# Expert stage: copying both halves of the next block's weights behind Silu and the gated product

## The chip, the cores and the metric

The kernel runs on one core of one Trainium2 chip. The metric is the device time of the whole program in microseconds, the median of the runs; the profile is that of one further execution. Engines are named as in the profile: PE is TensorE, DVE VectorE, ACT ScalarE, POOL GpSimd and SP SyncE, whose queue issues most transfers.

## The reference, cut to what matters

The program is one block of a hybrid model: four mixers over 1024 tokens of width 1024, and behind them a layer of 64 experts. The change is in the experts. A router picks 8 of 64 experts for each token. Each expert is a gated feed-forward with a hidden width of 256:

```python
def swiglu(t, wg, wu, wd):
    return (jax.nn.silu(t @ wg) * (t @ wu)) @ wd
```

`wg` and `wu` are 1024 x 256 (gate and up), `wd` is 256 x 1024 (down), all in float32. The tokens are sorted by expert and computed in blocks, and the results are weighted and summed per token later on.

## The kernel before

**Blocks.** The stage `experts` (L3086) works through 80 blocks (`NBLK`) of 128 rows. Each block has 4 sub-blocks of 32 rows, and each sub-block belongs to one expert, so a block can need the weights of up to four experts. Tables in SBUF, made from the routing in an earlier stage, give for each sub-block the ring slot of its gate and up weights, how many experts must have been loaded, and the ring slot of its down weights.

**Weights.** SyncE loads the experts in order into a ring of 3 slots for gate and up (2 MB per expert) and a ring of 4 for down (1 MB). It refills a gate-and-up slot once the copies out of it are done (`hi_d`, `hi_a`) and TensorE has read it (`up`). One sub-block of a block (number 3) is computed by TensorE straight from the ring. For the other three the weights are first copied within SBUF to fixed buffers (`WC`, `WDC`). The gate and up copies of a block are cut into a low half (contraction chunks 0 to 3) and a high half (chunks 4 to 7). VectorE copies sub-blocks 0 and 1 (L3408 and L3409 low, L3415 and L3416 high), ScalarE sub-block 2 (L3345 low, L3351 high). GpSimd copies the down weights of three sub-blocks (L3214) once TensorE has finished `widen` of the block before. There is one set of these buffers, so the low half may be overwritten only when TensorE is through the low chunks of the block that uses it (`half_up`), and the high half when it is through all of them (`up`).

**The engines' queues.** Every engine works in the order in which its code stands, and semaphores tie the engines together. For a step that ends block b0 and works on b1 behind it:

- TensorE (L3296): `hidden(b1)` makes the gate and up products of a block (L3253, L3255), 16 groups of four matmuls, with a wait for the high copies in front of its second eight; `widen(b0)` the down products (L3284, L3287); `fold(b1)` turns the hidden rows (L3270); `turn(b3)` turns the gathered rows of a later block (L3238). `hidden` also waits for the low copies and for the weights' arrival.
- ScalarE (L3353): `low(b2)`, `silu(b1)` (L3326), `high(b2)`, then `store(b0)` (L3331 and the store's issue at L3334), `fold(b1)` (L3338), and half of the scaled copies of turned rows, `flat_half(b3)` (L3320).
- VectorE (L3418): `low(b2)`, `gated(b1)` (L3396, Silu's result times the up product), `high(b2)`, `store(b0)` (L3401), `flat_half(b3)` (L3386), `index(b5)` (L3392).
- GpSimd (L3201): `copy_down` of the next block, then the indirect gather of rows of a later block (L3204), which waits for `index`.

`low` begins with register work: `slot_of` and `count_of` (L3117 to L3122) read the tables into registers of the engine, two slots and one count on VectorE, one of each on ScalarE. Then it waits for the experts' arrival and for `half_up`, and then it copies.
Of the kernel before, what the change touches and what calls it, by code (L numbers as in the profile page):

```python
# [63 lines left out]
def hold(eng, sem, value):  # L64

    eng.wait_ge(sem, value)
    if not isinstance(value, int):
        eng.nop(nofuse=True)  # L68
# [3017 lines left out]
def experts(nc, k, ctx, cr, wg, wu, wd, xn_dram, y_dram, TAB, END, IDX):  # L3086
# [30 lines left out]
    def slot_of(eng, b, u):  # L3117
        n = eng.value_load(TAB[0:1, bass.ds(b.n * SUB + u if u else b.n * SUB, 1)], min_val=0, max_val=RING - 1)
        return bass.ds(n, 1)

    def count_of(eng, b, u):
        return eng.value_load(TAB[0:1, bass.ds(b.n * SUB + (u + NTAB * P), 1)], min_val=1, max_val=NE)  # L3122
# [5 lines left out]
    def part_of(slot, cs):  # L3128
        return WGU[:, slot, :, cs, :].rearrange("p a g c n -> p (a g) (c n)")

    def copy_of(u, cs):
        return WC[:, u, :, cs, :].rearrange("p g c n -> p g (c n)")
# [7 lines left out]
    with nc.Block() as block:  # L3140
# [174 lines left out]
        @block.scalar  # L3315
        def _(act):
            def flat_half(b):
                hold(act, turned, b.n + 1)
                for c in range(KC // 2):
                    last = nc.scalar.activation(XTT[:, b.q, c], ps[0][:, c * P:(c + 1) * P], ACT.Identity,  # L3320
                                                bias=k.add_col[1][0][:, c:c + 1], scale=k.mul_col[1][0][:, c:c + 1])
                last.then_inc(xa, 1)

            def silu(b):
                hold(act, up, b.n + 2)
                nc.scalar.activation(SG[:, b.q], ps[2 + b.q][:, 0:ED], ACT.Silu).then_inc(sil, 1)  # L3326

            def store(b):
                hold(act, dn, b.n + 2)
                hold(act, st[b.q], b.half * 16 + 16)  # L3330
                nc.scalar.copy(YB[:, b.q, 0:512], ps[6][:, :]).then_inc(ya, 1)  # L3331
                hold(act, ya, b.n + 2)
                hold(act, yd, b.n + 2)
                act.dma_start(y_dram[bass.ds(b.n * P, P), :], YB[:, b.q]).then_inc(st[b.q], 16)  # L3334

            def fold(b):
                hold(act, ht, b.n + 1)
                nc.scalar.copy(HT[:, b.q], ps[4][:, 0:2 * P].rearrange("p (f n) -> p f n", f=2)).then_inc(hto, 1)  # L3338

            def low(b, n=1):  # L3340
                slot = slot_of(act, b, 2)
                hold(act, arrived, count_of(act, b, 2))
                if n:
                    hold(act, half_up, b.n)
                nc.scalar.copy(copy_of(2, LOW), part_of(slot, LOW)).then_inc(lo_a, 1)  # L3345
                return slot

            def high(b, slot, n=1):
                if n:
                    hold(act, up, b.n + 1)  # L3350
                nc.scalar.copy(copy_of(2, HIGH), part_of(slot, HIGH)).then_inc(hi_a, 1)  # L3351

            def step(b0, b1, b2, b3):  # L3353
                if b2 is not None:
                    slot = low(b2)
                silu(b1)
                if b2 is not None:
                    high(b2, slot)
                store(b0)
                fold(b1)  # L3360
                if b3 is not None:
                    flat_half(b3)

            high(Turn.at(0), low(Turn.at(0), 0), 0)
            flat_half(Turn.at(0))
            flat_half(Turn.at(1))
            slot = low(Turn.at(1))
            silu(Turn.at(0))
            high(Turn.at(1), slot)
            fold(Turn.at(0))  # L3370
            flat_half(Turn.at(2))
            with act.Fori(0, TRIPS - 1) as t:
                for off in range(2):
                    step(Turn(t, off), Turn(t, off + 1), Turn(t, off + 2), Turn(t, off + 3))
            for n in range(NBLK - 4, NBLK - 1):
                step(Turn.at(n), Turn.at(n + 1), *(Turn.at(n + d) if n + d < NBLK else None for d in (2, 3)))
            store(Turn.at(NBLK - 1))
            act.wait_ge(st[0], 16 * (TRIPS + 2))
            act.wait_ge(st[1], 16 * (TRIPS + 2))

        @block.vector
        def _(dve):
            def flat_half(b):
                hold(dve, turned, b.n + 1)
                for c in range(KC // 2, KC):
                    last = nc.vector.tensor_scalar(XTT[:, b.q, c], ps[1][:, (c - 4) * P:(c - 3) * P],  # L3386
                                                   k.mul_col[1][0][:, c:c + 1], k.add_col[1][0][:, c:c + 1],
                                                   ALU.mult, ALU.add)
                last.then_inc(xd, 1)

            def index(b):
                nc.vector.tensor_copy(ID[:, b.q], IDX[:, bass.ds(b.n, 1)]).then_inc(idx, 1)  # L3392

            def gated(b):
                hold(dve, sil, b.n + 1)
                nc.vector.tensor_tensor(H[:, b.q], SG[:, b.q], ps[2 + b.q][:, ED:], ALU.mult).then_inc(hid, 1)  # L3396

            def store(b):
                hold(dve, dn, b.n + 2)
                hold(dve, st[b.q], b.half * 16 + 16)  # L3400
                nc.vector.tensor_copy(YB[:, b.q, 512:], ps[7][:, :]).then_inc(yd, 1)  # L3401

            def low(b, n=1):
                slots = [slot_of(dve, b, u) for u in (0, 1)]
                hold(dve, arrived, count_of(dve, b, 1))
                if n:
                    hold(dve, half_up, b.n)
                nc.vector.tensor_copy(copy_of(0, LOW), part_of(slots[0], LOW))  # L3408
                nc.vector.tensor_copy(copy_of(1, LOW), part_of(slots[1], LOW)).then_inc(lo_d, 1)  # L3409
                return slots  # L3410

            def high(b, slots, n=1):
                if n:
                    hold(dve, up, b.n + 1)
                nc.vector.tensor_copy(copy_of(0, HIGH), part_of(slots[0], HIGH))  # L3415
                nc.vector.tensor_copy(copy_of(1, HIGH), part_of(slots[1], HIGH)).then_inc(hi_d, 1)  # L3416

            def step(b0, b1, b2, b3, b5):  # L3418
                if b2 is not None:
                    slots = low(b2)  # L3420
                gated(b1)
                if b2 is not None:
                    high(b2, slots)
                store(b0)
                if b3 is not None:
                    flat_half(b3)
                if b5 is not None:
                    index(b5)

            index(Turn.at(0))  # L3430
            index(Turn.at(1))
            high(Turn.at(0), low(Turn.at(0), 0), 0)
            flat_half(Turn.at(0))
            index(Turn.at(2))
            flat_half(Turn.at(1))
            index(Turn.at(3))
            slots = low(Turn.at(1))
            gated(Turn.at(0))
            high(Turn.at(1), slots)
            flat_half(Turn.at(2))  # L3440
            index(Turn.at(4))
            with dve.Fori(0, TRIPS - 1) as t:
                for off in range(2):
                    step(*(Turn(t, off + d) for d in (0, 1, 2, 3, 5)))
            for n in range(NBLK - 4, NBLK - 1):
                step(*(Turn.at(n + d) if n + d < NBLK else None for d in (0, 1, 2, 3, 5)))
            store(Turn.at(NBLK - 1))
# [202 lines left out]
```

## Time and profile before

| | us |
|---|---|
| median of 3 runs | 3009.71 (3006.03 to 3025.67) |
| the profiled execution | 3010.0 |
| its span | 3008.3 |
| TensorE matmul busy | 2621.9 (87%) |
| VectorE busy | 1537.0 (51%) |
| ScalarE busy | 983.5 (33%) |
| GpSimd busy | 829.3 (28%) |

The span runs from the first to the last instruction. Busy shares are averages over all stages; the expert stage covers the last third of the span but its end. Within it a line of the timeline is one instruction, or several of the same kind in a row, with its start counted from the start of the span. What an engine waited for stands in brackets.

### The profile page before, as it was taken

What the parts mean: (1) busy time and instruction counts of PE and PEld (TensorE: products, weight loads), DVE (VectorE), ACT (ScalarE), POOL (GpSimd) and SP (SyncE); (2) the same over time, 40 slices, a digit from 0 to 9 for tenths busy, and PEclk for the clock granted to TensorE, in tenths of its full rate; (3) what the DMA queues carried; (4) which work ended last, traced back from release to release, by engine and by line L of the source; (5) the groups of instructions that cost most, each with busy time, mean ns of one, the idle gap of its engine ahead of it and who ended that gap; (6) DMA issues with size and microseconds to landing.
All of it is one profiled execution on the core that took longest, in us unless ns stands there. A gap on an engine that the chain in (4) does not pass through costs nothing. (4 is left out here: it accounts for less than half of the span.)

```text
span 3008.3 us, 78943 instructions
## 1 busy us (share of the span) xinstructions
PE 2621.9 (87%) x30395; PEld 1471.1 (49%) x30396; DVE 1537.0 (51%) x2779; ACT 983.5 (33%) x1687; POOL 829.3 (28%) x654
## 2 busy tenths in 40 slices
PE   5998899798899698788969797898889998999956
PEld 2447368355788544788844352332333333333322
DVE  3116276553466504344444386565556655666628
ACT  3513127213222022222211113453445544555511
POOL 1000000001333000111100002565456555666565
PEclk9999999899999899999979898998999999999978
DMA  6001302300000100000022207787878887873167
GB/s 241 0 0 62 111 14 85 102 15 1 3 4 4 51 18 1 3 4 4 4 100 84 102 8 286 286 313 289 310 300 317 315 303 292 304 286 145 77 268 319
DMA packets 109130, 408.57 MB, mean 136 GB/s; under 512 B 21001, under 2 KB 37083, under 8 KB 83932
## 3 DMA queue, kind: packets, MB, share of 16 engines
q1 hardware_dynamic: 76636, 287.71, 26.2%
q0 software_dynamic: 20736, 75.51, 6.6%
q10 hardware_dynamic: 11520, 41.95, 3.5%
q8 instruction: 178, 2.92, 0.4%
q14 instruction: 60, 0.49, 0.0%
HBM read 346.40 MB, written 58.72 MB: 135 GB/s over the span
## 5 line engine op out<-in xcount | busy, mean ns | idle before, releaser
L3253 PE MATMUL bank<-arena 128*32 x1280 | 584.0, 611 | 45.7 <-SPq L68 36.1
L3255 PE MATMUL bank<-arena 128*32 128x512 f32 x3840 | 585.1, 611 | 0.0
L3214 POOL COPY arena<-arena 128x2048 f32 x240 | 456.4, 1935 | 392.3 <-PE bank L3287 390.8
L1341 PE MATMUL bank<-arena 64*64 64x64 f32 x8320 | 279.1, 220 | 69.7 <-DVE arena L1437 19.7
L3253 PEld LDWEIGHTS bank<-arena 128*32 128x32 f32 x1280 | 137.3, 112 | 408.6 <-issue 400.7
L1341 PEld LDWEIGHTS bank<-arena 64*64 64x64 f32 x8320 | 261.8, 136 | 81.5 <-DVE arena L1437 22.4
L3284 PE MATMUL bank<-arena 128*32 x640 | 290.3, 597 | 5.5 <-POOL arena L3214 5.5
L3287 PE MATMUL bank<-arena 128*32 128x512 f32 x1920 | 291.3, 597 | 0.0
L3408 DVE COPY arena<-arena 128x2048 f32 x80 | 130.7, 1633 | 262.2 <-PE bank L3255 204.6
L3345 ACT COPY arena<-arena 128x2048 f32 x80 | 152.0, 1901 | 277.2 <-PE bank L3255 160.0
L3204 POOL DMA_INDIRECT arena<-normed_rows,arena x80 | 152.4, 1906 | 163.5 <-DVE arena L3392 152.1
L3284 PEld LDWEIGHTS bank<-arena 128*32 128x32 f32 x640 | 70.6, 110 | 198.8 <-issue 198.7
L3255 PEld LDWEIGHTS bank<-arena 128*32 128x32 f32 x3840 | 152.7, 112 | 0.0
L3351 ACT COPY arena<-arena 128x2048 f32 x80 | 151.9, 1899 | 0.0
L2478 POOL TENSOR_TENSOR arena<-arena 128x512 f32<-128x512 f32 x10 | 12.8, 1283 | 463.5 <-DVE arena L2536 463.5
L1435 DVE TENSOR_TENSOR arena<-arena,bank 128x512 f32<-128x512 f32 x100 | 68.8, 688 | 123.9 <-PE bank L1341 115.7
L1575 PE MATMUL bank<-arena 128*128 128x512 f32 (+1 forms) x320 | 129.5, 565 | 0.3 <-PE bank L1575 0.3
L3386 DVE TENSOR_SCALAR arena<-bank,arena 128x128 f32<-128x128 f32 x320 | 109.2, 403 | 36.8 <-PE bank L3238 36.8
L497 PE MATMUL bank<-arena 128*128 128x512 f32 (+1 forms) x320 | 127.3, 552 | 0.0
L2748 PE MATMUL bank<-arena 128*128 128x512 f32 x256 | 115.0, 608 | 9.7 <-ACT arena L2770 8.5
L3320 ACT ACTIVATE arena<-bank,arena 128x128 f32<-128x128 f32 x320 | 120.8, 465 | 3.3 <-PE bank L3238 3.3
L1456 DVE SCALAR_TENSOR_TENSOR arena<-arena 128x945 f32<-128x945 f32 (+2 forms) x96 | 113.8, 1220 | 1.7
(561 smaller groups left out, 4438.9 us busy)
## 6 DMA issues: line engine op xcount, KB each, us to landing
arena<-in_exp_w_gate_dram SPq DMA_DIRECT2D x64, 1024.0 KB
arena<-in_exp_w_up_dram SPq DMA_DIRECT2D x64, 1024.0 KB
arena<-in_exp_w_down_dram SPq DMA_DIRECT2D x64, 1024.0 KB
expert_rows<-arena ACTq DMA_DIRECT2D x80, 512.0 KB
arena<-in_w_mod_dram SPq DMA_DIRECT2D x32, 512.0 KB, 9.8
arena<-in_x_dram SPq DMA_DIRECT2D x16, 512.0 KB, 7.7
arena<-in_w_mod_dram SPq DMA_DIRECT2D x8, 1024.0 KB, 17.7
arena<-in_w_in_dram SPq DMA_DIRECT2D x12, 384.0 KB
```

Of the source, the lines that this page charges most:

```text
L497: last = nc.tensor.matmul(k.ps[p % 4][:, 0:width], k.hT[:, c, t * P:(t + 1) * P], W[g][:, c, ws], start=(c == 0), stop=(c == KC - 1))
L1341: last = self.nc.tensor.matmul(self.banks[bank][r, x * HD:(x + 1) * HD], lhsT[r, x], rhs[r, x], start=True, stop=True)
L1575: last = nc.tensor.matmul(k.ps[p % 4][:, 0:w], W[m // 3 % 2][:, c, (m % 3) * P:(m % 3 + 1) * P], k.hT[:, c, a:a + w], start=(c == 0), stop ...
L3204: nc.gpsimd.indirect_dma_start(out=G[:, b.q], out_offset=None, in_=xn_dram, in_offset=bass.IndirectOffsetOnAxis(ap=ID[:, b.q], axis=0)).th ...
L3214: last = nc.gpsimd.tensor_copy(down_copy(u), down_of(slots[u]))
L3253: nc.tensor.matmul(out(SUB - 1), XTT[:, b.q, c, rows(SUB - 1)], W[:, :, c], start=first, stop=end)
L3255: last = nc.tensor.matmul(out(u), XTT[:, b.q, c, rows(u)], WC[:, u, :, c], start=first, stop=end)
L3284: nc.tensor.matmul(ps[6 + half][rows(SUB - 1), :], HT[:, b.q, f, rows(SUB - 1)], W[:, f, c], start=(f == 0), stop=(f == 1))
L3287: last = nc.tensor.matmul(ps[6 + half][rows(u), :], HT[:, b.q, f, rows(u)], WDC[:, u, f, c], start=(f == 0), stop=(f == 1))
L3345: nc.scalar.copy(copy_of(2, LOW), part_of(slot, LOW)).then_inc(lo_a, 1)
L3351: nc.scalar.copy(copy_of(2, HIGH), part_of(slot, HIGH)).then_inc(hi_a, 1)
L3408: nc.vector.tensor_copy(copy_of(0, LOW), part_of(slots[0], LOW))
```

## The change

On both engines the step called `low(b2)` first, kept the slots it returned, did `silu(b1)` or `gated(b1)`, and then called `high(b2, slots)`. Now `silu(b1)` or `gated(b1)` comes first, and `high(b2, low(b2))` behind it. The same is done in front of the loop. What `low` and `high` do is unchanged: the register reads, the waits and the copies move together.

```diff
@@ ScalarE
             def step(b0, b1, b2, b3):
-                if b2 is not None:
-                    slot = low(b2)
                 silu(b1)
                 if b2 is not None:
-                    high(b2, slot)
+                    high(b2, low(b2))
                 store(b0)
                 fold(b1)
@@
-            slot = low(Turn.at(1))
             silu(Turn.at(0))
-            high(Turn.at(1), slot)
+            high(Turn.at(1), low(Turn.at(1)))
             fold(Turn.at(0))
@@ VectorE
             def step(b0, b1, b2, b3, b5):
-                if b2 is not None:
-                    slots = low(b2)
                 gated(b1)
                 if b2 is not None:
-                    high(b2, slots)
+                    high(b2, low(b2))
                 store(b0)
@@
-            slots = low(Turn.at(1))
             gated(Turn.at(0))
-            high(Turn.at(1), slots)
+            high(Turn.at(1), low(Turn.at(1)))
             flat_half(Turn.at(2))
```

## Rows read from the trace of the kernel before

**Rows 1.** TensorE's timeline: start us, us, engine, line, operation, count

```profile
1845.45 1.06 PE L3253 MATMUL bank<-arena 128*32 x1
...
2246.34 0.62 PE L3253 MATMUL bank<-arena 128*32 x1
...
2249.80 0.59 PE L3253 MATMUL bank<-arena 128*32 x1
...
2252.81 0.60 PE L3255 MATMUL bank<-arena 128*32 128x512 f32 x3
...
2258.11 0.62 PE L3253 MATMUL bank<-arena 128*32 x1
...
2858.33 0.62 PE L3253 MATMUL bank<-arena 128*32 x1
```

**Rows 2.** Waits in the expert stage: us in total, times, longest us

```profile
PE bank L3253 <- SPq L68: 36.1, 6, 9.6
...
PE bank L3270 <- DVE arena L3396: 17.3, 5, 6.6
```

**Rows 3.** TensorE's timeline behind two gaps

```profile
2015.86 0.61 PE L3253 MATMUL bank<-arena 128*32 x1 [1.66 <-issue]
...
2367.19 0.61 PE L3253 MATMUL bank<-arena 128*32 x1 [3.07 <-SPq L68]
...
2368.06 1.05 PE L3253 MATMUL bank<-arena 128*32 x1
```

**Rows 4.** Busy time by window: us, PE, PEld, DVE, ACT, POOL, PEclk, DMA share, GB/s

```profile
2369.00:2371.00 2.00, 2.00 (x16) 0.58 (x12) 0.00 (x0) 0.00 (x0) 0.80 (x1) 0.50 0.88 324
```

**Rows 5.** VectorE's timeline in the step of rows 1

```profile
2250.23 1.83 DVE L3408 COPY arena<-arena 128x2048 f32 x1 [2.27 <-PE bank L3255]
...
2254.03 0.42 DVE L3396 TENSOR_TENSOR arena<-arena,bank 128x256 f32<-128x256 f32 x1 [0.84 <-ACT arena L3326]
2254.37 1.22 DVE L3415 COPY arena<-arena 128x2048 f32 x1
2255.50 1.22 DVE L3416 COPY arena<-arena 128x2048 f32 x1
...
2259.58 0.15 DVE L3392 COPY arena<-arena 128x1 int32 x1
```

**Rows 6.** ScalarE's timeline in the same step

```profile
2250.20 1.90 ACT L3345 COPY arena<-arena 128x2048 f32 x1 [1.77 <-PE bank L3255]
2253.55 0.38 ACT L3326 ACTIVATE arena<-bank 128x256 f32<-128x256 f32 x1 [1.45 <-PE bank L3255]
```

**Rows 7.** GpSimd's timeline in the same step

```profile
2257.11 5.56 POOL L3214 COPY arena<-arena 128x2048 f32 x3 [3.79 <-PE bank L3287]
```

**Rows 8.** VectorE's queue, first and last register record of three steps; ns min/median/max

```profile
L3118 DVEq ALU_OP  x1: 40/40/40, 2247.3 to 2247.3; - x1
L3122 DVEq SEQ_ASSERT  x1: 23/23/23, 2249.9 to 2249.9; - x1
...
L3118 DVEq ALU_OP  x1: 40/40/40, 2294.4 to 2294.4; - x1
L3122 DVEq SEQ_ASSERT  x1: 23/23/23, 2296.5 to 2296.5; - x1
...
L3118 DVEq ALU_OP  x1: 40/40/40, 2497.1 to 2497.1; - x1
L3122 DVEq SEQ_ASSERT  x1: 23/23/23, 2500.7 to 2500.7; - x1
```

**Rows 9.** Timeline: GpSimd's and VectorE's copies side by side; a late copy

```profile
1849.56 7.55 POOL L3214 COPY arena<-arena 128x2048 f32 x3 [1.52 <-SPq L3185]
...
2038.63 2.82 DVE L3408 COPY arena<-arena 128x2048 f32 x1 [9.38 <-SPq L68]
...
2501.05 1.23 DVE L3408 COPY arena<-arena 128x2048 f32 x1 [3.25 <-issue]
```

**Rows 10.** SyncE's waits in the expert stage: us in total, times, longest

```profile
SPq L68 <- DVE arena L3416: 21.5, 3, 7.7
```

## The prediction, made before the changed kernel was run

> **What bounds the kernel now.** I read the groups by line first: the costliest lines belong to the expert stage. Then the stage's ends: TensorE's first product of the first block starts at 1845.45, that of the last of 80 blocks at 2858.33, so 79 steps from block to block take 1012.9 us [rows 1]. Then one undisturbed step, engine by engine. `hidden` starts at 2246.34 and again at 2258.11, 11.77 us later, and TensorE has no gap in between: 7.07 us of `hidden` to the end of its last products (2252.81 + 0.60 = 2253.41), then `widen`, `fold`, `turn` [rows 1]. A step is TensorE's; 79 x 11.77 = 929.8 us. The other 83.1 us lie in steps whose weights came late. The list of waits has 36.1 us of them as TensorE waiting for the queue that announces weights [rows 2]; the slow clock behind a gap is another part [rows 3, 4].
>
> I count time from the end of `hidden` (2253.41 = 0). VectorE's low copies start at -3.18, behind the first half of `hidden`; ScalarE's Silu at 0.14, VectorE's gated product at 0.62, its high copies at 0.96, done at 3.31 [rows 5, 6]. GpSimd's three copies start at 3.70 and take 5.56 [rows 7]. `hidden` of the next block starts at 4.70 and wants the low copies then, the high ones 3.46 later (its ninth group, 2249.80 against 2246.34), at 8.16 [rows 1]. Now the high copies are 4.85 us early, the low ones as much or more.
>
> **The change part by part.** No instruction is added; one wait, on the first half of `hidden`, is asked later and is then always met. Moved is `low`: two copies on VectorE, one on ScalarE, and the register work ahead of them (reads of slot numbers and counts from the table). The queues of TensorE, GpSimd and SyncE keep their order.
>
> *Silu and gated product* start where they do now, since they wait for the end of `hidden`. `fold` comes at 3.4, so in an undisturbed step an earlier product brings nothing. With late weights it does: TensorE waited 17.3 us in 5 steps for a product [rows 2], held up behind late low copies. That is all there is to gain.
>
> *Register work.* VectorE's runs from 2247.3 to 2249.9, 2.6 us, under the idle time before its copy, which starts 0.33 later at 2250.23 [rows 5, 8]. In another step it took 2.1 us, in a third 3.6 us; in this third VectorE stood idle for 3.25 us with only this to wait for, and the copy started 0.35 behind its last record [rows 8, 9]. After the change the work stands behind the wait for Silu and starts about with the gated product, beside its 0.42 us. Bounds 2.1 and 3.6; I take 2.6, the length in the step I follow. The first low copy asks at 0.62 + 2.6 + 0.33 = 3.55.
>
> *Copies beside GpSimd's.* A VectorE copy alone takes 1.22 us, the next one starting 1.13 behind it [rows 5]. Beside GpSimd's it took 2.82, and GpSimd's three took 7.55 for 5.56 [rows 7, 9]. Turn by turn fits both: a GpSimd copy is 5.56 / 3 = 1.85, and one of VectorE's behind it some 1.0, together 2.85; three of GpSimd's with two of VectorE's between them are 5.56 + 2.0 = 7.56. So I take it that whichever asks first goes first. Sharing in proportion would make every VectorE copy last 2.85 from 3.70 on: low copies done near 9.1, `hidden` from 9.2, a step of 9.2 + 7.07 + 1.7 for the clock (below) = 18.0.
>
> The Trainium skill ("SBUF — State Buffer", Who interferes with whom) says that a VectorE copy of this kind and a GpSimd operation exclude each other for a whole instruction, the one that issues first going first. By that rule, the trace agrees, with the 7.55; a model of shared bandwidth would give the 18.0.
>
> By turns: the first low copy asks at 3.55, before GpSimd's 3.70, and ends at 4.68. Then GpSimd and VectorE alternate: second low copy done at 7.53, high ones at 10.38 and 13.23; GpSimd's last at 12.23.
>
> *TensorE.* `hidden` starts at 7.6 for 4.70, a gap of 2.9. Its first half ends at 7.6 + 3.46 = 11.1 and waits for the high copies to 13.23; with 0.14 for the handover, as Silu shows [rows 6], it resumes at 13.4, and the second half takes 3.61 (2249.80 to 2253.41) [rows 1]. The next end is at 17.0: a step grows by 5.23.
>
> *TensorE's clock.* Behind a gap of 3.07 us the granted clock fell to 0.50, the 1.2 GHz level, and groups took 1.05 us for 0.59; there are four such, 0.85 apart for 0.43, so 1.7 us [rows 3, 4]. Behind a gap of 1.66 the group that starts `hidden` took its usual 0.61 [rows 3]. The new gap is near the upper one. If the clock falls, the first half ends at 12.8, still ahead of 13.4: I cost it at nothing. Its cover is the wait for the high copies; without that it is 1.7 per step.
>
> *ScalarE.* Silu to 0.5, register work, two copies of 1.90 [rows 6]: even with 3.6 us of register work both end by 8.3, inside VectorE's 13.23. Its store issue waits for VectorE's store at about 14, and the folded hidden rows behind that, by 15, are wanted by `widen` at 17.0. It holds.
>
> *Tails.* VectorE's store, scaled copies and index end 3.0 behind the high copies (2259.58 + 0.15 against 2256.72) [rows 5], near 16.3 and so before the next 17.0. GpSimd's gather waits for that index instead of following its copies at once; its rows are wanted two steps later. Nothing.
>
> *Weights.* SyncE refills a slot once its high copies are done, now 10 us later in a step. It has waited for them in 3 places only, 21.5 us in all [rows 10]: refills set their own pace, and blocks now come 5 us slower. Of the 83.1 us of late weights between 0 and 83.1 stay. I take 10: the lower end is nearer, but several small experts in a row can still outrun three slots.
>
> *Sum:* 79 x 5.23 = 413, less 83.1 - 10 = 73: +340 us. On the profiled execution (3010.0 us, span 3008.3; 0.3 from the median, 3009.7) that is **3350 us**.
>
> **Rivals.**
> 1. *GpSimd first.* With 2.75 us or more of register work the first low copy asks after 3.70. Low copies are then done at 6.55 and 9.40, high ones at 12.25 and 13.4; `hidden` starts at 9.5, a gap of 4.8, and its end is at 9.5 + 7.07 + 1.7 = 18.3. 79 x 6.5 - 73 = +440: 3450 us. For it: a margin of only 0.15, and a step with 3.6 us. Against it: the 2.1 [rows 8]. Chance 0.20. Sharing in proportion gives 79 x 6.2 - 73 = +417, 3427 us; against it stands the 7.56 for 7.55. Chance 0.06.
> 2. *Register work half hidden* (0.8 to 1.9 us). Both low copies are through before 3.70, and the first high copy waits for GpSimd: high ones done at 3.70 + 2 x 2.85 = 9.4 for 8.16, a step of 13.2. 79 x 1.4 = 111, less some 70 of weight waits: 3050 us. No step that I read shows under 2.1. Chance 0.10.
> 3. *The other side: register work for nothing.* If it were done while VectorE waits for Silu, low copies would run from 1.05, the first high copy would ask ahead of 3.70, and the last would end at 7.4, before 8.16. It decides at a first low copy at 1.4. Steps stay 11.77, and the 17.3 us go: 2993 us. For it: the queue runs half a microsecond ahead of the engine, whose index copy of that step comes 11.77 before 2259.58, at 2247.8, behind the start of the register work at 2247.3 [rows 5, 8]. Against it: a wait stands ahead of it now. Chance 0.08, 0.02 of it for more than 1% faster.
> 4. *Worse:* the clock stays low in the second half too, or weights are as late as before on top of rival 1: over 3480. Chance 0.06.
>
> **How the numbers follow.** The forecast has 0.50; its own range is 3310 (register work 2.1, all 0.5 earlier: 79 x 0.5 = 40) to 3420 (all 83 us of weight waits stay). The range, 3240 to 3480, adds rival 1 and sharing; the lower end leaves room for an order that alternates with rival 2's. Left out are rivals 2 to 4, some 0.2. Within 1% (30 us, about what a measurement of this kernel can tell from no change) lies most of rival 3 alone: faster 0.02, same 0.06, slower 0.92.
>
> **What would show it.** First low copy at 3.5 behind the end of `hidden`, the reads behind the gated product; three of VectorE's four copies at 2.8 or more, GpSimd's three at 8.5 with the wait for the first; TensorE waiting 2.9 us ahead of `hidden` and 2.2 in its middle; steps of 17.0; hardly a wait for weights. It is wrong if the register work is over before 1.4, or if copies beside GpSimd's are not slowed; and by 100 us if GpSimd asks first.

## The result and the profile after

The changed kernel takes 3334.16 us (median of 4 runs, 3326.61 to 3341.46) against 3011.41 before: a ratio of 1.1065, 95% interval 1.1037 to 1.1092. The forecast was 3350 us. All the readings in this section are of the profiled execution, 3338.48 us with a span of 3336.8. One execution of one version below (one slot ahead) ran in a slow state, at 4617 us against 3157 to 3163 of its other three, and is left out of that version's time.

The page shows VectorE busy for 1867.6 us, 330.6 more than before, with the same number of instructions, and GpSimd for 935.9, 106.6 more; TensorE is busy for 2691.5. The groups of the page say where. The columns are those of the page: busy us and mean ns of one, then the idle time ahead of them and what ended it.

```profile
L3253 PE MATMUL bank<-arena 128*32 x1280 | 650.2, 659 | 317.6 <-DVE arena L3406 223.6
L3214 POOL COPY arena<-arena 128x2048 f32 x240 | 635.9, 2684 | 364.6 <-PE bank L3287 363.1
...
L3412 DVE COPY arena<-arena 128x2048 f32 x80 | 229.3, 2867 | 0.0
L3413 DVE COPY arena<-arena 128x2048 f32 x80 | 229.2, 2865 | 0.0
L3406 DVE COPY arena<-arena 128x2048 f32 x80 | 224.6, 2807 | 0.0
...
L3405 DVE COPY arena<-arena 128x2048 f32 x80 | 98.2, 1227 | 168.3 <-issue 156.2
```

The first low copy (L3405) takes 1.23 us, as a copy does alone. The other three take 2.81 to 2.87, and a copy of GpSimd's 2.68 for 1.85. In front of the first low copy VectorE stood idle for 156.2 us with nothing to wait for, 2.0 us a time: that is the register work. TensorE, which had no gap in an undisturbed step, stood idle for 317.6 us in front of `hidden` and within it.

One step shows it in order of time. VectorE's timeline:

```profile
2331.56 0.42 DVE L3393 TENSOR_TENSOR arena<-arena,bank 128x256 f32<-128x256 f32 x1 [2.79 <-ACT arena L3326]
2334.01 1.23 DVE L3405 COPY arena<-arena 128x2048 f32 x1 [2.03 <-issue]
2335.16 2.91 DVE L3406 COPY arena<-arena 128x2048 f32 x1
2337.99 2.91 DVE L3412 COPY arena<-arena 128x2048 f32 x1
2340.82 2.91 DVE L3413 COPY arena<-arena 128x2048 f32 x1
```

GpSimd's copies in that step:

```profile
2334.59 8.05 POOL L3214 COPY arena<-arena 128x2048 f32 x3 [4.11 <-PE bank L3287]
```

TensorE's timeline with the end of one `hidden` (its last group, started at 2330.21, ends at 2330.81) and the first and ninth group of the next:

```profile
2330.21 0.59 PE L3253 MATMUL bank<-arena 128*32 x1
...
2338.64 0.61 PE L3253 MATMUL bank<-arena 128*32 x1 [3.05 <-DVE arena L3406]
...
2344.08 0.61 PE L3253 MATMUL bank<-arena 128*32 x1 [1.80 <-DVE arena L3413]
```

Counted from the end of `hidden`, 2330.81: the product at 0.75, the first low copy at 3.20, GpSimd at 3.78, the second low copy done at 7.26, `hidden` from 7.83 instead of 4.70 [rows 1], the high copies done at 12.92. TensorE waits twice, 3.05 us and 1.80 us. The step from 2321.75, where the `hidden` before began, to 2338.64 is 16.89 us. Over the stage, `hidden` of the first block starts at 1845.18 and that of the last at 3184.51:

```profile
1845.18 1.05 PE L3253 MATMUL bank<-arena 128*32 x1
...
2321.75 0.61 PE L3253 MATMUL bank<-arena 128*32 x1 [2.76 <-DVE arena L3406]
...
3184.51 1.06 PE L3253 MATMUL bank<-arena 128*32 x1 [2.92 <-DVE arena L3406]
```

That is 1339.3 us for 79 steps, 326.4 more than before, of the 328.5 by which the two spans differ. The whole loss lies in the steps. The waits of the stage (us in total, times, longest) say what became of late weights. The first line is the wait ahead of `hidden`, the second the one in its middle, as far as the trace assigns it:

```profile
PE bank L3253 <- DVE arena L3406: 223.6, 75, 3.4
PE bank L3253 <- DVE arena L3413: 82.2, 46, 2.0
...
PE bank L3253 <- SPq L68: 9.1, 1, 9.1
```

TensorE's waits for the queue that announces weights fell from 36.1 us in 6 places [rows 2] to 9.1 in one. SyncE, on the other hand, waits far more for the high copies than before (21.5 us in 3 places [rows 10]), and hardly anyone waits for SyncE: the weights come faster than the blocks. From SyncE's list:

```profile
SPq L68 <- DVE arena L3413: 294.9, 38, 20.8
```

### The profile page after: what moved, and what is told of

Read it like the earlier page. It is cut to its first block and busy times, and to the rows that moved or that the text cites. A ratio compares the mean times of both kernels' runs of the same rounds, so it can differ in the third digit from the quotient of the medians.

```text
span 3336.8 us, 78905 instructions
## 1 busy us (share of the span) xinstructions
PE 2691.5 (81%) x30395; PEld 1474.4 (44%) x30396; DVE 1867.6 (56%) x2779; ACT 977.3 (29%) x1687; POOL 935.9 (28%) x654
## 3 DMA queue, kind: packets, MB, share of 16 engines
q8 instruction: 178, 2.92, 0.3%
## 5 line engine op out<-in xcount | busy, mean ns | idle before, releaser
L3253 PE MATMUL bank<-arena 128*32 x1280 | 650.2, 659 | 317.6 <-DVE arena L3406 223.6
L3214 POOL COPY arena<-arena 128x2048 f32 x240 | 635.9, 2684 | 364.6 <-PE bank L3287 363.1
L3255 PE MATMUL bank<-arena 128*32 128x512 f32 x3840 | 652.7, 659 | 0.0
L3284 PE MATMUL bank<-arena 128*32 x640 | 290.0, 596 | 8.1 <-POOL arena L3214 5.5
L3287 PE MATMUL bank<-arena 128*32 128x512 f32 x1920 | 291.1, 596 | 0.0
L3412 DVE COPY arena<-arena 128x2048 f32 x80 | 229.3, 2867 | 0.0
L3413 DVE COPY arena<-arena 128x2048 f32 x80 | 229.2, 2865 | 0.0
L3406 DVE COPY arena<-arena 128x2048 f32 x80 | 224.6, 2807 | 0.0
L3338 ACT COPY arena<-bank 128x256 f32<-128x256 f32 x80 | 29.8, 372 | 642.9 <-DVE arena L3398 642.9
L3204 POOL DMA_INDIRECT arena<-normed_rows,arena x80 | 77.3, 966 | 416.0 <-DVE arena L3389 415.7
L3405 DVE COPY arena<-arena 128x2048 f32 x80 | 98.2, 1227 | 168.3 <-issue 156.2
L3393 DVE TENSOR_TENSOR arena<-arena,bank 128x256 f32<-128x256 f32 x80 | 33.7, 421 | 246.9 <-ACT arena L3326 246.9
L1575 PE MATMUL bank<-arena 128*128 128x512 f32 (+1 forms) x320 | 129.6, 565 | 0.3 <-PE bank L1575 0.3
## 6 DMA issues: line engine op xcount, KB each, us to landing
arena<-in_w_mod_dram SPq DMA_DIRECT2D x8, 1024.0 KB, 18.3
```

Of the source, the lines that this page charges most:

```text
L1575: last = nc.tensor.matmul(k.ps[p % 4][:, 0:w], W[m // 3 % 2][:, c, (m % 3) * P:(m % 3 + 1) * P], k.hT[:, c, a:a + w], start=(c == 0), stop ...
L3214: last = nc.gpsimd.tensor_copy(down_copy(u), down_of(slots[u]))
L3253: nc.tensor.matmul(out(SUB - 1), XTT[:, b.q, c, rows(SUB - 1)], W[:, :, c], start=first, stop=end)
L3255: last = nc.tensor.matmul(out(u), XTT[:, b.q, c, rows(u)], WC[:, u, :, c], start=first, stop=end)
L3284: nc.tensor.matmul(ps[6 + half][rows(SUB - 1), :], HT[:, b.q, f, rows(SUB - 1)], W[:, f, c], start=(f == 0), stop=(f == 1))
L3287: last = nc.tensor.matmul(ps[6 + half][rows(u), :], HT[:, b.q, f, rows(u)], WDC[:, u, f, c], start=(f == 0), stop=(f == 1))
```

## The experiments

Theory A is the prediction's: the register work, moved behind the product, pushes VectorE's copies into the time of GpSimd's, and from there the two engines take turns, the one that asks first going first. All versions but two are made from the changed kernel; ScalarE's half alone and the last one are made from the kernel before. Times of the steps are medians over the steps of the profiled execution. The first low copy's start, the time at which GpSimd asks for its first copy, and the end of the last high copy are counted from the end of `hidden`.

| version | first low copy | GpSimd asks | high done | step | program | ratio to before |
|---|---|---|---|---|---|---|
| before | -3.2 | 3.7 | 3.3 | 11.8 | 3011 | 1 |
| all reads ahead | 1.0 | 3.8 | 7.3 | 12.0 | 3026.19 | 1.0032 (1.0019 to 1.0045) |
| two slots ahead | 1.6 | 3.8 | 8.8 (7.9 or 9.6) | 13.6 | 3072.04 | 1.0185 (1.0146 to 1.0223) |
| one slot ahead | 2.3 | 3.8 | 10.3 | 14.3 | 3158.90 | 1.0483 (1.0434 to 1.0532) |
| changed kernel | 3.2 | 3.8 | 12.9 | 16.9 | 3334.16 | 1.1065 (1.1037 to 1.1092) |
| VectorE later | 4.3 | 3.7 | 13.5 | 19.5 | 3523.25 | 1.1684 (1.1654 to 1.1714) |
| GpSimd later | 3.2 | 4.8 | 11.2 | 15.2 | 3208.35 | 1.0641 (1.0614 to 1.0669) |

Where reads or copies are moved, the diffs below show the lines in one engine's step; the same is done in front of the loop. `look_up` does the reads, and `low` then takes what it found.

**All reads ahead.** Only the register reads go back in front of Silu and the product, on both engines (the diff has VectorE's step); the copies stay where the change put them.

```diff
             def step(b0, b1, b2, b3, b5):
+                if b2 is not None:
+                    found = look_up(b2)
                 gated(b1)
                 if b2 is not None:
-                    high(b2, low(b2))
+                    high(b2, low(b2, 1, found))
```

> The changed kernel, but the register reads of slots and counts stand ahead of Silu and the gated product again; only the copies stay behind them. Theory A (the reads behind the product push the first low copy to about GpSimd's start, and from there the two engines take turns): without them the first low copy starts at about 1.05 us after the end of hidden, the first high copy asks ahead of GpSimd, the high copies are done by about 7.4, steps are 11.8 us again, and the program takes 2990 to 3020 us. Rival B (copies are slowed in proportion while GpSimd copies, whoever asks first): high copies done near 8.4, steps of 12.1, some 3030 us. Rival C (the copies are simply too late behind the product, and the reads hardly matter): steps near 16.9 and 3300 us or more.

3026.19 us, 1.0032 of the kernel before. VectorE's and GpSimd's timelines:

```profile
2417.43 0.42 DVE L3399 TENSOR_TENSOR arena<-arena,bank 128x256 f32<-128x256 f32 x1 [5.50 <-ACT arena L3326]
2417.76 1.22 DVE L3414 COPY arena<-arena 128x2048 f32 x1
2418.90 1.22 DVE L3415 COPY arena<-arena 128x2048 f32 x1
2420.04 1.22 DVE L3421 COPY arena<-arena 128x2048 f32 x1
2421.17 2.91 DVE L3422 COPY arena<-arena 128x2048 f32 x1
```

```profile
2420.51 7.16 POOL L3214 COPY arena<-arena 128x2048 f32 x3 [3.98 <-PE bank L3287]
```

The order that the change wanted, product first and both halves behind it, costs 10 us (3026.19 against 3015.89 for the kernel before on the same chip) instead of 323. The third copy asks 0.47 us ahead of GpSimd and goes through; only the fourth waits. The high copies are done at 7.3, as expected, before the 8.16 at which TensorE wants them. Rivals B and C fall. The program came out 6 us above the range of A: the gain that A allowed for late weights did not come, and steps are 12.0 us and not 11.77. Where these 0.2 us lie was not followed.

**One half of the change each.** VectorE's half alone (ScalarE copies its low half first, as before; the diff below), and ScalarE's alone (the kernel before with ScalarE's part of the change):

```diff
             def step(b0, b1, b2, b3):
-                silu(b1)
                 if b2 is not None:
-                    high(b2, low(b2))
+                    slot = low(b2)
+                silu(b1)
+                if b2 is not None:
+                    high(b2, slot)
```

> Only VectorE's half of the change: ScalarE copies its low half first, as before. Theory A: all of the loss is VectorE's, 3320 to 3345 us, steps of 16.9. Rival D (ScalarE's copy, now behind Silu, carries part of it): about halfway, near 3170 us.

> Only ScalarE's half of the change: VectorE copies its low half first, as before. Theory A: ScalarE's copies end by 6 us after the end of hidden and hide behind everything, so 2990 to 3020 us, at best 17 us under the kernel before, where Silu no longer stands behind a late low copy. Rival D: near 3170 us.

ScalarE's half alone takes 3024.13 us (1.0020, 1.0003 to 1.0037): it costs next to nothing, as A says, and brings nothing. But VectorE's half alone takes 3427.26 us (1.1355, 1.1333 to 1.1377), 93 us more than both together, where A and D allowed no more than 3345. Its steps alternate between 16.4 to 17.9 and 19.1 us. ScalarE's timeline in a step of 19.1, behind an end of `hidden` at 2596.7:

```profile
2593.53 0.35 ACTq L3334 DMA_DIRECT2D expert_rows<-arena  x1
...
2596.32 1.90 ACT L3345 COPY arena<-arena 128x2048 f32 x1 [0.55 <-issue]
2598.12 0.38 ACT L3326 ACTIVATE arena<-bank 128x256 f32<-128x256 f32 x1
```

ScalarE can issue its store only behind VectorE's, which now comes some 13.5 us after the end of `hidden`. Its own low copy and the reads before it therefore end late, and Silu, which stands behind the copy, starts 1.4 us after the end of `hidden` instead of 0.14. VectorE's timeline and GpSimd's in the same step:

```profile
2598.60 0.42 DVE L3396 TENSOR_TENSOR arena<-arena,bank 128x256 f32<-128x256 f32 x1 [3.96 <-ACT arena L3326]
2601.05 2.31 DVE L3408 COPY arena<-arena 128x2048 f32 x1 [2.03 <-issue]
```

```profile
2600.39 7.55 POOL L3214 COPY arena<-arena 128x2048 f32 x3 [4.02 <-PE bank L3287]
```

The first low copy asks 0.66 us behind GpSimd and loses the first turn: it is rival 1 of the prediction, in every second step (38 of 78; in 36 of them Silu started 0.9 us or more after the end of `hidden`). So ScalarE's half of the change is not free of effect: with VectorE's half in place it keeps Silu on time, and is worth 93 us.

**GpSimd's copies cut short.** This version leaves out most of the copying of the down weights: from the second block on, 128 of 2048 columns are copied, so the results are not those of the block, and only the time is of use.

```diff
+                c = slice(0, 128 if n else 2 * D)
                 for u in range(SUB - 1):
-                    last = nc.gpsimd.tensor_copy(down_copy(u), down_of(slots[u]))
+                    last = nc.gpsimd.tensor_copy(down_copy(u)[:, c], down_of(slots[u])[:, c])
```

> The changed kernel with GpSimd's copies of the down weights cut from 2048 to 128 columns per partition from the second block on (most of that work is left out). Theory A: VectorE's four copies all take 1.22 us, low ones done at 5.5 after the end of hidden, high ones at 7.8, steps of 12.6 us, 79 x 4.3 = 340 us less, with some waits for weights back: 3000 to 3050 us. Rival E (the later start alone costs the time, GpSimd has no part in it): 3300 us or more.

3086.22 us (two runs): 248 us less than the changed kernel, and 36 above the range. VectorE's four copies start at 3.1 and are done at 8.0, TensorE's wait in the middle is gone, and steps are 13.3 us. The 0.7 us over the expected 12.6 are an error of mine in the expectation: I took `hidden` to start as soon as the low copies end (5.5) but it starts at 6.2, some 0.6 us behind their end, as in the changed kernel. Of the 5.1 us per step GpSimd's part is therefore 16.9 - 13.3 = 3.6, and 1.5 remain for the later start alone. Rival E falls for the larger part and holds for that rest.

**Who asks first.** GpSimd made later by two more reads, and VectorE made later by two more:

```diff
                 if n:
                     hold(pool, dn, b.n + 1)
+                    for u in range(2):
+                        down_slot_of(pool, b, u)
```

```diff
                 if n:
                     hold(dve, half_up, b.n)
+                    for u in (0, 1):
+                        slot_of(dve, b, u)
```

> The changed kernel with two more register reads on GpSimd between its wait for the end of widen and its copies, so that it asks about 0.9 us later, at 4.6 us instead of 3.7 after the end of hidden. Theory A (turns; whoever asks first goes first): VectorE's second low copy asks at 4.3, ahead of GpSimd, low copies are done at 5.4, one copy of GpSimd's fewer stands before each later one, the high copies are done at 11.1, steps are 15.1 us and the program takes 3334 - 79 x 1.8 = 3190 us: faster through more work. Rival B (slowed in proportion): steps of 16.0, 3260 us. Rival E (GpSimd has no part): no change, 3334 us.

> The changed kernel with two more register reads on VectorE in front of its low copies, about 1.2 us, so that the first low copy asks at 4.4 us instead of 3.2 after the end of hidden, behind GpSimd's 3.7. Theory A: GpSimd goes first, low copies are done at 6.6 and 9.4, hidden starts at 9.5 with a gap that costs the clock 1.7 us, steps are 18.3 us: 3334 + 79 x 1.4 = 3445 us. Rival B (in proportion): low copies done at 10.1, steps of 19.0, 3500 us. Rival E (everything is simply moved by the added reads): 16.9 + 1.2 = 18.1, 3430 us; what tells it from A is the first low copy, 2.8 us in A and 1.2 in E.

*GpSimd later:* 3208.35 us, 126 us less than the changed kernel though each step does more. VectorE's timeline and GpSimd's:

```profile
2492.33 1.23 DVE L3407 COPY arena<-arena 128x2048 f32 x1 [2.01 <-issue]
2493.48 1.22 DVE L3408 COPY arena<-arena 128x2048 f32 x1
2494.61 2.91 DVE L3414 COPY arena<-arena 128x2048 f32 x1
2497.44 2.91 DVE L3415 COPY arena<-arena 128x2048 f32 x1
```

```profile
2494.06 8.04 POOL L3216 COPY arena<-arena 128x2048 f32 x3 [5.13 <-issue]
```

The second low copy is at work when GpSimd asks, and takes 1.22 us to its end, unslowed. With sharing in proportion (B) it would have slowed. The step is 15.2 us, against 15.1 in A and 16.0 in B, and the program 18 us above A's 3190 and 52 under B's 3260.

*VectorE later:* 3523.25 us. VectorE's first low copy and GpSimd's copies in one step:

```profile
2632.13 2.44 DVE L3407 COPY arena<-arena 128x2048 f32 x1 [3.27 <-issue]
```

```profile
2631.60 7.55 POOL L3214 COPY arena<-arena 128x2048 f32 x3 [5.16 <-PE bank L3287]
```

The first low copy asks at 4.3, behind GpSimd, and takes 2.44 us, in all 78 steps over 2 us. So GpSimd did go first and E falls. But A's 3445 us is 78 too low, and the time is nearer to B's 3500. The copies are A's, with the low ones done at 9.5 (9.4 in A, 10.1 in B) and the high ones at 13.5; the steps are 19.5 us and not the 18.3 of A. The rest is TensorE's timeline:

```profile
2637.98 1.06 PE L3253 MATMUL bank<-arena 128*32 x1 [5.40 <-DVE arena L3408]
2638.83 1.06 PE L3253 MATMUL bank<-arena 128*32 x1
...
2641.39 1.06 PE L3253 MATMUL bank<-arena 128*32 x1
2642.25 0.79 PE L3253 MATMUL bank<-arena 128*32 x1
```

Behind the gap of 5.40 us the first five groups take 1.06 us and start 0.85 apart, and a sixth is part slow: 5 x 0.42 + 0.2 = 2.3 us (1.3 to 2.9 in other steps), where I took 1.7 from the kernel before; and `hidden` starts at 10.1 for 9.5, of which the handover is again 0.57.

**Part of the reads ahead.** Two slot reads ahead of the product and the count behind it (the diff below); and one slot ahead, one and the count behind:

```diff
             def step(b0, b1, b2, b3, b5):
+                if b2 is not None:
+                    slots = look_up(b2)
                 gated(b1)
                 if b2 is not None:
-                    high(b2, low(b2))
+                    high(b2, low(b2, 1, slots))
```

> The changed kernel with VectorE's two slot reads ahead of the gated product; only the read of the count stays between the product and the copies. The first low copy should start at about 1.7 us after the end of hidden, between 0.95 (all reads ahead) and 3.2 (none). Theory A (turns): the low copies are through by 4.0, GpSimd has asked at 3.75, so the first high copy waits for one of its copies and the second for another: high ones done near 9.7 us, TensorE's wait moves from in front of hidden into its middle alone, steps of 13.6 us; with some 40 us of weight waits, 3115 us. Rival F (the loss grows evenly with the delay of the copies, 137 us per us of delay): 3129 us. The total does not tell them apart; the high copies do: 2.9 us each and done at 9.7 in A, at 8.1 in F (7.3 + 0.8).

> The same with one slot read ahead, one slot and the count behind: first low copy at about 2.4 us. Theory A (turns): both low copies have asked before GpSimd (second at 3.55, GpSimd at 3.75), so the count of turns is the same as with two slots ahead and everything is only 0.7 us later: high ones done at 10.4, hidden from 5.3, steps of 14.3 us, 3155 us. The step from here to the changed kernel is then the large one (180 us for 0.8 us of delay), since there the second low copy has lost its place. Rival F (evenly with the delay): 3225 us.

3072.04 and 3158.90 us. VectorE's and GpSimd's timelines with two slots ahead:

```profile
2450.00 1.23 DVE L3408 COPY arena<-arena 128x2048 f32 x1 [0.57 <-issue]
2451.14 1.22 DVE L3409 COPY arena<-arena 128x2048 f32 x1
2452.28 2.92 DVE L3415 COPY arena<-arena 128x2048 f32 x1
2455.12 2.91 DVE L3416 COPY arena<-arena 128x2048 f32 x1
```

```profile
2452.09 4.86 POOL L3214 COPY arena<-arena 128x2048 f32 x2 [4.02 <-PE bank L3287]
```

Here the third copy asks 0.19 us behind GpSimd and takes 2.92; with all reads ahead it asked 0.47 us ahead and took 1.22. With two slots ahead the order in fact falls both ways, and that is the sharpest test of who goes first. Of 78 steps, the third copy took 1.22 us in 39, and in each of these its record starts ahead of GpSimd's or at most 0.02 us behind it; in the other 39 it starts 0.03 us or more behind, and takes 2.9. The high copies are done at 7.9 in the first kind and at 9.6 in the second, and from one end of `hidden` to the next it is 12.1 and 13.6 us. So A's 13.6 us and 9.7 hold for half of the steps only. Rival F has the high copies done at 8.1 in every step and gives no two kinds. The shorter steps are worth 39 x 1.5 = 60 us, which is more than the 43 by which the program is faster than its sum. In them GpSimd asks at 4.1 (median) instead of 3.7; why was not followed.

With one slot ahead there is one kind only: the third copy is slow in all 78 steps, steps are 14.3 us and the high copies done at 10.3, as A had them (14.3 and 10.4), and the program is 4 us from its sum and 66 from rival F's.

From -3.2 to 1.0 the delay of the first low copy costs 0.2 us per step. From there on the high copies end later by the delay itself and, for each VectorE copy that has lost its turn, by another 1.7 us (starts 2.83 apart for 1.13): 7.3 with one such copy, 9.6 with two, 10.3 with two and 0.7 of delay, 12.9 with three. With VectorE later there are still three, since GpSimd has three copies; but now both low ones are among them, so `hidden` starts 2.3 us later, and the slow groups behind the longer gap are no longer covered by a wait in its middle.

**A version better than both?** ScalarE's half alone with its reads ahead of Silu.

```diff
             def step(b0, b1, b2, b3):
+                if b2 is not None:
+                    found = look_up(b2)
                 silu(b1)
                 if b2 is not None:
-                    high(b2, low(b2))
+                    high(b2, low(b2, 1, found))
```

> Only ScalarE's half of the change, and ScalarE's register reads ahead of Silu; VectorE as before. It is a candidate for a version better than both. In an undisturbed step nothing changes (11.77). Where weights are late, Silu and the product no longer stand behind ScalarE's late copy: up to 17 us of TensorE's waits for the product go. Theory A: 2990 to 3012 us. If those waits only turn into waits for the same weights: 3011 us, no change.

3020.78 us, a ratio of 1.0017 (0.9999 to 1.0034): no change, as the expectation's second case has it. None of the nine versions beats the kernel before. The 17.3 us that TensorE waited for late products [rows 2] are not to be had this way. In this run it waits for the same weights at another place: in the step from 1918.1 `hidden` of the next block starts 17.4 us behind the end of the one before. That these waits only move was argued from a few steps and not tried by itself.

## Why the prediction was right

*What bounds a step, and what covers the copies.* Right. Steps of 11.8 us became steps of 16.9 (17.0 forecast), 77 of 78 between 15.1 and 17.8, and TensorE waits ahead of `hidden` and in its middle. With the reads back in front the loss was 10 us instead of 323.

*Register work, 2.6 us.* The mechanism was right, the size 0.5 too large: in the changed kernel it runs from 2331.6 to 2333.7, the lower bound of 2.1, with reads of 0.30 to 0.32 us, so the first low copy asks at 3.2 and not at 3.55. Over all 78 steps it took 1.8 to 2.3 us, median 2.1, where the kernel before has 1.4 to 3.6 and a median of 2.6: the 2.6 was a fair reading of the kernel before, and the work got shorter with its new place. The margin to GpSimd was 0.6 us and not 0.15, and rival 1 did not come in any step of the changed kernel. That it did not is the lucky side of this term, since nothing in the rows said that the long reads would be gone. It came in every second step of VectorE's half alone, and in all of them with two more reads.

*Turns beside GpSimd.* Right, and the best supported part: three of four copies at 2.9, high ones done at 12.9 for 13.23. GpSimd's three copies took 8.05 for the 8.53 of the sum (3.70 to 12.23), since they had 0.4 less to wait for VectorE's first. The rule of the Trainium skill ("SBUF — State Buffer", Who interferes with whom) holds in the order as well: whoever issues first keeps its full speed, seen in a third copy at 1.22 us when 0.47 ahead and at 2.92 when 0.19 behind, and in the 39 and 39 steps with two slots ahead.

*TensorE's handovers.* 0.1 us ahead of `hidden` and 0.14 in its middle were too small: measured 0.57 (2335.16 + 2.91 = 2338.07, start at 2338.64) and 0.35 (2343.73, start at 2344.08). They are terms of the sum in their own right, and they made up for the shorter register work: 7.26 + 0.57 = 7.83 against 7.53 + 0.1, and 12.92 + 0.35 against 13.23 + 0.14.

*TensorE's clock at nothing.* Right for most steps, but the cover was thinner than the sum had it. Behind 42 of the 72 gaps of 2.5 to 3.3 us no group was slow at all. Behind 16, four or five were, and the wait in the middle took up their 1.7 us, as forecast. In 13 steps seven were slow, all in the first half of `hidden`, and cost 2.7 to 2.9 us. One of them:

```profile
3014.04 1.05 PE L3253 MATMUL bank<-arena 128*32 x1 [3.06 <-DVE arena L3406]
...
3018.30 1.06 PE L3253 MATMUL bank<-arena 128*32 x1
3019.16 0.93 PE L3253 MATMUL bank<-arena 128*32 x1
```

The granted clock from 3014.5 to 3018.5 was 0.50, the 1.2 GHz level. There the first half ran past the arrival of the high copies, the wait in the middle was gone, and `hidden` took 9.7 to 9.9 us for 9.1: some 0.8 us each and 10 us in all. Where the gap was long and no wait stood in the middle, with VectorE later, it cost all that it costs alone, and more than I had taken.

*Weights, 10 us left of 83.* The stage holds 1339.3 - 79 x 16.9 = 4 us beyond its median steps, with one wait of 9.1 us for weights and the 10 us of slow groups above, and some steps shorter than the median. Right in kind; the lower end was nearer still.

*ScalarE.* "It holds" was right for the whole change, but I had missed that it holds only because `low` moved on ScalarE too. Had I priced VectorE's half by itself, I would have got 3350 instead of 3427.

*The rivals' prices.* Rival 2 was priced too low. Its ground, a first low copy some 1.7 to 2.8 us behind the end of `hidden`, is what the versions with slots ahead have (1.6 and 2.3). The prediction has both low copies through before 3.7 there. In fact the second had asked by then and was through at 4.0 and 4.7. The programs took 3072 and 3159 us, where the prediction has one price of 3050. Rival 3's ground is that of all reads ahead: 12.0 us and 3026, where it has 11.77 and 2993, since the 17.3 us did not go.

The sum was 16 us above the median. The mechanism was forecast; that the size came out so near is in part luck, since the register work, both handovers and the slow groups were off by up to half a microsecond or more a time and cancelled to 0.1 us per step.

## What to carry to other kernels

When copies are moved behind another step, their register reads move with them, and these (2.0 us here) can decide on whose turn the copies fall. Where VectorE's and GpSimd's copies can meet, work out who asks first at each of them: here 0.03 us of order decided over 1.7 us of one copy, and 1 us of added work on the right engine gained 126 us in the program. And price each engine's half of a change alone; here one half cost some 410 us, the other 8, and both together 323.

## What the runs showed of the hardware beyond this

- The wait that leads TensorE into `hidden` took 0.57 us from the end of VectorE's copy to the first product; the one in the middle took 0.35 us. Behind the first, three more waits stand in TensorE's queue, behind the second one. That these make the difference was not tried. Silu started 0.14 behind TensorE [rows 6].
- VectorE's slot reads took 0.30 to 0.32 us in the step of the changed kernel shown above (median of all 160 0.31, longest 0.56); before, the median was 0.37 us and the longest 1.4 us. What slows them was not tried.
- The length of a gap ahead of `hidden` does not by itself say what the clock costs. In the changed kernel 72 gaps were between 2.5 and 3.3 us: 42 had no slow group behind them, the others four, five or seven, for 1.7 to 2.9 us. With VectorE later, one of 5.40 us cost 2.3.
- Even copies of 128 columns on GpSimd took 3.2 us for three beside VectorE's, since each had to wait for its turn (the first, beside the tail of one VectorE copy, 0.72 us, the next two 1.28 and 1.29); VectorE's took 1.31 for 1.22 beside them.
